# The first two attention tiles on shared weight slots, and the first loads in order

## The reference

```
h   = RMSNorm(x)
one projection of h: q, f, i, g (4 x 512), attention q, k, v (512, 128, 128), two gates (2 x 1024)
A   = HGRN2: S_t = diag(f_t) S_(t-1) + k_t v_t^T, o_t = S_t^T q_t, 4 heads of 128;
      per-head RMS norm, times silu(g)
B   = causal attention over a window of 128, 8 heads of 64 on 2 key heads,
      QK norm, ALiBi, a sink logit in the denominator
x1  = x + (sigmoid(gate_a) * (A @ w_a) + sigmoid(gate_b) * (B @ w_b)) @ w_out
y   = x1 + (gelu(conv3(gate)) * val) @ w_down,   gate, val = RMSNorm(x1) @ w_up  (2 x 2816)
```

## Time and profile before

| | us |
|---|---|
| Runs of the kernel before | 3895.78, 4335.41, 3762.58 (median 3895.78) |
| Profiled execution, time | 3760.1 |
| Its span, slowest of 8 cores | 3758.6 (fastest 3747.6) |
| TensorE busy | 3604.0 (96%) |
| ScalarE, VectorE, POOL busy | 2128.2, 2046.0, 520.6 |
| Moved by DMA | 742.35 MB |

### The profile page before, as it was taken

How to read it: one execution, slowest core, us unless ns; L and a number is a source line. 1 busy time by engine, 2 the same in 40 slices (tenths; PEclk the granted TensorE clock), 3 DMA queues, 4 the chain that set the end, 5 groups by cost and what they waited for, 6 DMA issues and landing times.

```text
span 3758.6 us, 64664 instructions; the slowest of 8 cores (3747.6 to 3758.6 us)
## 1 busy us (share of the span) xinstructions
PE 3604.0 (96%) x21154; PEld 1968.3 (52%) x21516; DVE 2046.0 (54%) x3275; ACT 2128.2 (57%) x3595; POOL 520.6 (14%) x1176
## 2 busy tenths in 40 slices
PE   5779999999999999999999999999999999999999
PEld 2334645546455464654646455464554646456466
DVE  4355455564555646556565555645556465555544
ACT  5567374664746647365483745747375483755722
POOL 1203112010120201102011020201202011020100
PEclk9899999999999999999999999999999999999999
DMA  8879969847465564655646465474655646566464
GB/s 188 180 225 201 258 180 243 257 157 249 143 227 189 181 228 153 222 177 194 225 157 228 161 227 194 159 251 157 205 188 192 230 156 215 178 203 212 136 227 147
DMA packets 205814, 742.35 MB, mean 198 GB/s; under 512 B 22832, under 2 KB 23216, under 8 KB 205488
## 3 DMA queue, kind: packets, MB, share of 16 engines
q1 hardware_dynamic: 191088, 687.95, 54.3%
q0 software_dynamic: 13536, 48.24, 8.2%
q10 hardware_dynamic: 864, 2.00, 0.2%
HBM read 687.76 MB, written 98.57 MB: 209 GB/s over the span
## 4 chain that ended last, share of the span: by engine, by line
PE 86%; ACT 6%; issue 3%; DMA 3%; DVE 1%; POOL 0%; ACTq 0%; another core or an unknown queue 0%; DVEq 0%; SPq 0%; POOLq 0%
PE bank L652 86%; ACT fa L608 2%; DMA wF<-wscr 1%; ACT ef L608 1%; ACT L608 1%; ACT xs L609 1%; DMA wA<-wscr 1%; DMA gB<-c_g 0%; ACT ba L608 0%; DVE fa L630 0%; DMA wF<-wall 0%; DVE ef L625 0%; DMA wA<-wall 0%; PE bank L660 0%; ACT hT L608 0%
## 5 line engine op out<-in xcount | busy, mean ns | idle before, releaser
L652 PE MATMUL bank<-h2T,wF 128*128 128x512 bf16 x5520 | 1282.0, 379 | 40.1 <-ACT ef L608 22.7
L652 PE MATMUL bank<-hT,wA 128*128 128x512 bf16 x4069 | 963.1, 381 | 24.8 <-DMA wA<-wscr 8.4
L652 PEld LDWEIGHTS bank<-h2T,wF 128*128 128x128 bf16 x5632 | 537.0, 98 | 692.4 <-issue 81.3
L625 DVE SCALAR_TENSOR_TENSOR ef<-bank,cft,ef 128x512 f32<-128x512 f32 x704 | 520.7, 747 | 311.8 <-ACT ef L608 265.4
L652 PEld LDWEIGHTS bank<-hT,wA 128*128 128x128 bf16 x4224 | 408.6, 98 | 473.1 <-issue 28.7
L652 PE MATMUL bank<-wF,act 128*128 128x256 bf16 x5632 | 648.9, 273 | 4.2 <-DMA wF<-wscr 4.2
L652 PEld LDWEIGHTS bank<-wF,act 128*128 128x128 bf16 x5632 | 549.1, 98 | 104.0 <-issue 5.5
L608 ACT ACTIVATE ef<-bank,cft 128x512 f32<-128x512 f32 x352 | 273.4, 777 | 327.3 <-PE bank L652 264.4
L630 DVE TENSOR_TENSOR act<-ef,bank 128x512 bf16<-128x512 f32 x352 | 241.5, 686 | 360.4 <-PE bank L652 351.1
L608 ACT ACTIVATE ef<-ef 128x512 f32<-128x512 f32 x352 | 215.4, 627 | 207.4 <-DVE ef L625 205.5
L608 ACT ACT_TABLE_LOAD x235 | 301.5, 1283 | 47.3 <-PE bank L652 31.7
(11 more groups left out here) (87 smaller groups left out, 3358.0 us busy)
## 6 DMA issues: line engine op xcount, KB each, us to landing
wF<-wscr SPq DMA_DIRECT2D x430, 512.0 KB, 4.6
wA<-wscr SPq DMA_DIRECT2D x396, 512.0 KB, 4.9
xt<-x SPq DMA_DIRECT2D x128, 512.0 KB, 7.6
x1scr<-xt SPq DMA_DIRECT2D x64, 512.0 KB, 4.5
xt<-x1scr SPq DMA_DIRECT2D x64, 512.0 KB, 5.8
x<-x1scr SPq DMA_DIRECT2D x64, 512.0 KB, 8.2
y<-x SPq DMA_DIRECT2D x64, 512.0 KB, 6.0
wF<-wall POOLq DMA_DIRECT2D x50, 512.0 KB, 11.8
```

Of the source, the lines that this page charges most:

```text
L625: return P.record("dve", lambda h: h.scalar_tensor_tensor(out=res(out), in0=res(in0), scalar=scalar, in1=res(in1), op0=op0, op1=op1), read ...
L652: inst = h.matmul(res(out), lhsT=res(lhsT), rhs=res(rhs), start=st, stop=sp_)
```

## The change

- Tiles 0 and 1 of stage A use the same weight slots: `load_piece` gives tile 1 the buffer that tile 0 loaded. Tile 1's instructions get priorities from 0.2 on instead of from 1.
- Tile 1's stage A keeps its state in buffers of the MLP (`h2T`, `act`, the x1 pool), as `set1`. `kn` and `vtz` exist twice and alternate. Stage F of tile 0 is recorded after stage A of tile 1, and so on, one behind.
- All pieces of A are copied to `wscr` in tile 0. Of the last four pieces of A three are loaded in tile 0 into the buffers `ef` of the MLP, right after the first gate piece.
- First loads: only cf, cbb and gB0 stay on ScalarE's queue; gB1, mask and dm go to SP's queue, behind certain weight loads. The first two casting loads wait until the first and the second x block have landed.
- Planner: stage A may hold 5 banks instead of 6, `foff` is 0.3 instead of 0.2, priority runs by TensorE cost instead of by count, the small tiles (`sm`) are 6 instead of 5, the score matmuls are costed in full; kt is allocated and recorded ahead of sT.

```diff
-CAPS = dict(pA=6, pF=5)
-TUNE = dict(nxt=4, nxs=4, nwa=5, nwf=5, dA=18, dF=10, dF2=99, rF=1, skew=4, gc=0, foff=0.2, hold=6000.0)
+CAPS = dict(pA=5, pF=5)
+TUNE = dict(xw=1, we=1, le=0, lf=2, nsm=6, rx=0, lj=5, lc=4, a1=0.2, sw=0, gx=0, pm=1.0, dw=1e9, nxt=4, nxs=4, nwa=5, nwf=5, dA=18, dF=10, dF2=99, rF=1, skew=4, gc=0, foff=0.3, hold=6000.0)
...
+            if kind == "A" and ti == 1:
+                base = TUNE["a1"]
+            tot = sum(o.cost for o in ops if o.eng == "pe") or 1.0
+            cum = 0.0
+            m = TUNE["pm"]
             for i, o in enumerate(ops):
-                o.prio = base + i / n
+                o.prio = base + (1.0 - m) * i / n + m * cum / tot
+                if o.eng == "pe":
+                    cum += o.cost
...
-        kn = sb("kn", [128, NB + 1, 128], BF16)
-        vtz = [sb(f"vtz{i}", [128, NB + 1, 128], BF16) for i in range(2)]
+        kn2 = [sb(f"kn{i}", [128, NB + 1, 128], BF16) for i in range(2)]
+        vtz2 = [[sb(f"vtz{i}{j}", [128, NB + 1, 128], BF16) for i in range(2)] for j in range(2)]
...
-        cload("gB1", gB[1][:], c_g[1], 524288)
-        cload("mask", mask_st[:], c_mask, 65536)
-        cload("dm", dm[:], c_dm.rearrange("p a b g t -> p a b (g t)"), 524288)
...
+        set0 = (hT, bhT, qs, bqs, gs, bgs, kd, bkd, vtm, bvtm, qn, bqn, mixT, bmix, gbuf, bgb)
+        set1 = (h2T, bh2T, act[:, 16:20, :], bact[16:20], x1v[0], alias[0], x1v[1], alias[1], x1v[2], alias[2], x1v[3], alias[3],
+                act[:, 0:8, :], bact[0:8], act[:, 8:16, :], bact[8:16])
...
-        keep_at = [(1 if i >= TUNE["dA"] else 0) if p["kind"] == "A" else (2 if i - na >= TUNE["dF2"] else 1 if i - na >= TUNE["dF"] else 0) for i, p in enumerate(pieces)]
+        keep_at = [0 if p["kind"] == "A" else (2 if i - na >= TUNE["dF2"] else 1 if i - na >= TUNE["dF"] else 0) for i, p in enumerate(pieces)]
...
+        def late_const(name):
+            if name == ("q", 0):
+                cload("mask", mask_st[:], c_mask, 65536, eng="sp")
+                P.ops[-1].deps.add(lds[("f", 1)])
+                cload("dm", dm[:], c_dm.rearrange("p a b g t -> p a b (g t)"), 524288, eng="sp")
+            elif name == ("gab", 0):
+                cload("gB1", gB[1][:], c_g[1], 524288, eng="sp")
+                P.ops[-1].deps.add(lds[("g", 1)])
+
         def load_piece(ti, kind, name):
+            if ti == 0:
+                late_const(name)
+            if kind == "A" and ti == 1:
+                return shared[name]
...
+            early = ti == 0 and name in (("wo", 1), ("wo", 2), ("wo", 3)) and TUNE["we"]
+            w = vb(pEF if early else pool, f"w{kind}{ti}_{name}")
...
+            if ti == 0 and name in (("f", 0), ("f", 1)):
+                o_.deps.add(xld[0 if name[1] == 0 else int(TUNE["xw"])])
+            if early:
+                after(o_, lds[("gab", int(TUNE["le"]))])
...
+            hT, bhT, qs, bqs, gs, bgs, kd, bkd, vtm, bvtm, qn, bqn, mixT, bmix, gbuf, bgb = set1 if ti == 1 else set0
+            kn, bkn, vtz, bvtz = kn2[par], bkn2[par], vtz2[par], bvtz2[par]
...
-        for ti in range(ntile):
+        stage_a(0)
+        stage_a(1)
+        stage_f(0)
+        for ti in range(2, ntile):
             stage_a(ti)
-            stage_f(ti)
+            stage_f(ti - 1)
+        stage_f(ntile - 1)
```

More of the change, by code:

```diff
@@ L54 @@
 class VBuf(Buf):
-    __slots__ = ("pool", "slot", "left", "users", "end", "rsv", "cls")
+    __slots__ = ("pool", "slot", "left", "users", "end", "rsv", "cls", "pre")
     def __init__(self, pool, name, rsv=0, cls=""):
@@ L61, in __init__ @@
         self.pool = pool
+        self.pre = ()
         self.slot = None
@@ L68, in __getitem__ @@
     def __getitem__(self, k):
-        return Lz(self, (("g", k),))
+        return Lz(self, self.pre + (("g", k),))
     def lz(self):
@@ L245, in schedule @@
                     st = o.ready
+                    if o.nbytes and dma_free - TUNE["dw"] > st:
+                        st = dma_free - TUNE["dw"]
                     ok = True
@@ L584, in build_program @@
         pBA = mkpool("ba", 6, [T], BF16)
-        pSM = mkpool("sm", 5, [4, 128], BF16)
+        pSM = mkpool("sm", int(TUNE["nsm"]), [4, 128], BF16)
         pEF = mkpool("ef", 3, [2, T + 1], F32)
@@ L720, in build_program @@
         bS32 = mk("S32")
-        bkn = [mk(f"kn{b}") for b in range(NB + 1)]
-        bvtz = [mk(f"vt{b}") for b in range(NB + 1)]
+        bkn2 = [[mk(f"kn{b}") for b in range(NB + 1)] for j in range(2)]
+        bvtz2 = [[mk(f"vt{b}") for b in range(NB + 1)] for j in range(2)]
         bdd = [mk("dd0"), mk("dd1")]
@@ L728, in build_program @@
         for i_ in range(2):
-            P.record("pool", lambda h, i_=i_: h.memset(vtz[i_][:], 1.0), [], bvtz, 700.0)
+            for j_ in range(2):
+                P.record("pool", lambda h, i_=i_, j_=j_: h.memset(vtz2[j_][i_][:], 1.0), [], bvtz2[j_], 700.0)
         for j in range(2):
@@ L745, in build_program @@
         bgd = [mk("gd0"), mk("gd1")]
+        x1v = [a.bitcast(BF16).rearrange("p (a n) -> p a n", a=4) for a in pX1.aps]
+        alias = [[[mk(f"gsx{h}_{b}") for b in range(NB)] for h in range(4)], [mk(f"kdx{h}") for h in range(4)],
+                 [mk(f"vtmx{b}") for b in range(NB)], [[mk(f"qnx{j}_{b}") for b in range(NB)] for j in range(4)]]
+        set0 = (hT, bhT, qs, bqs, gs, bgs, kd, bkd, vtm, bvtm, qn, bqn, mixT, bmix, gbuf, bgb)
+        set1 = (h2T, bh2T, act[:, 16:20, :], bact[16:20], x1v[0], alias[0], x1v[1], alias[1], x1v[2], alias[2], x1v[3], alias[3],
+                act[:, 0:8, :], bact[0:8], act[:, 8:16, :], bact[8:16])
+        x1_users = []
         bgsum = mk("gsum")
@@ L751, in build_program @@
         first_f = {}
+        shared = {}
         na = sum(1 for p in pieces if p["kind"] == "A")
-        keep_at = [(1 if i >= TUNE["dA"] else 0) if p["kind"] == "A" else (2 if i - na >= TUNE["dF2"] else 1 if i - na >= TUNE["dF"] else 0) for i, p in enumerate(pieces)]
-        last_ld = {}
+        keep_at = [0 if p["kind"] == "A" else (2 if i - na >= TUNE["dF2"] else 1 if i - na >= TUNE["dF"] else 0) for i, p in enumerate(pieces)]
+        lds = {}
+        xld = []
         bx1 = {}
@@ L762, in load_piece @@
             pool = pWA if kind == "A" else pWF
-            w = vb(pool, f"w{kind}{ti}_{name}")
+            early = ti == 0 and name in (("wo", 1), ("wo", 2), ("wo", 3)) and TUNE["we"]
+            w = vb(pEF if early else pool, f"w{kind}{ti}_{name}")
+            if early:
+                w.pre = (("r", ("p a n -> p (a n)", {})), ("b", BF16))
             nk = sum(l[3] for l in p["loads"]) if p["loads"][0][3] == 4 and len(p["loads"]) == 2 else p["loads"][0][3]
@@ L766, in load_piece @@
             size = nk * cols
+            if kind == "A" and ti == 0:
+                shared[name] = w
             at = keep_at[i]
@@ L771, in load_piece @@
             o_ = DMA(w[:, 0:size], wall[i, :, 0:size], [], [w], w, size * 512, eng="pool")
-            P.link("al" + kind, o_)
-            last_ld[kind] = o_
+            P.link("alE" if early else "al" + kind, o_)
+            lds[name] = o_
+            if ti == 0 and name in (("f", 0), ("f", 1)):
+                o_.deps.add(xld[0 if name[1] == 0 else int(TUNE["xw"])])
+            if early:
+                after(o_, lds[("gab", int(TUNE["le"]))])
             if kind not in first_f:
@@ L776, in load_piece @@
                 if kind == "F":
-                    after(o_, last_ld["A"])
+                    after(o_, lds[("gab", int(TUNE["lf"]))])
             if ti == at and ntile > at + 1:
@@ L783, in bank, with norm_block @@
             return VBuf(pr[0], "ps", pr[1], pr[2])
-        def norm_block(which, b, xv, hdst, bhdst, pool):
+        def norm_block(ti, which, b, xv, hdst, bhdst, pool):
             st4 = nst[which]
@@ L806, in stage_a @@
             par = ti % 2
+            hT, bhT, qs, bqs, gs, bgs, kd, bkd, vtm, bvtm, qn, bqn, mixT, bmix, gbuf, bgb = set1 if ti == 1 else set0
+            kn, bkn, vtz, bvtz = kn2[par], bkn2[par], vtz2[par], bvtz2[par]
+            kn_o, bkn_o, vtz_o, bvtz_o = kn2[1 - par], bkn2[1 - par], vtz2[1 - par], bvtz2[1 - par]
             for b in range(NB):
@@ L810, in stage_a @@
                 o_ = DMA(xv.lz(), x_d[r0:r0 + 128, :], [], [xv], xv, 524288, chain="xn")
-                after(o_, lead.get(("A", ti - 1)))
+                xld.append(o_)
+                if ti != 1:
+                    after(o_, lead.get(("A", ti - 1)))
                 after(o_, gate.get(ti - int(TUNE["skew"])))
-                norm_block(0, b, xv, hT, bhT, pPA)
+                norm_block(ti, 0, b, xv, hT, bhT, pPA)
             if ti > 0:
-                CP("pool", kn[:, 0, :], kn[:, NB, :], [bkn[NB]], [bkn[0]], n=128)
+                CP("pool", kn[:, 0, :], kn_o[:, NB, :], [bkn_o[NB]], [bkn[0]], n=128)
                 for kv in range(2):
                     vs = slice(kv * 64, (kv + 1) * 64)
```

(29 more changed lines are left out.)

## The result

The changed kernel takes 3788.87 us (median of four runs, 3784.25 to 3793.61). Against the kernel before, each by its comparable runs, the ratio is 1.0075, 95% interval 1.005 to 1.0099: slower, though within 2%. The profiled execution has a span of 3782.7 us, 24 us more than before; I had forecast 3708.

The account below looks back on a forecast made before the run. TensorE bounds the kernel, busy 3604.0 of 3758.6 us. Sixteen steady periods (3629.3 us) plus 19 + 29 + 10 + 10 + 6 + 5 = 79 instead of 129 give span 3708, time 3710 us; range 3675 to 3780.

Parts of the forecast that it names:

- I take 0: Steady periods: the planner's other edits change nothing; ends -1.3 and +5 us a period.
- (d): MLP tiles 0 and 1, 265 to 860 us: idle 10 us above steady instead of 14; ends 5 and 25.
- (a): Start: gB0 at 11 us instead of 18.8, first projection at 23 us instead of 32.98, a gain of 10.
- Rival 2: Steady periods worsen: stage A's bank cap makes TensorE wait in the block part; at 6 us a period 3794; chance 0.1.
- (b): Pair of attention tiles after the first projection: idle 32 us, 29 above steady, against 46; ends 7 and 54.
- My 260 among the signs: Sign for the pair: TensorE busy about 87% from the first projection to 260 us, clock 0.95 or more.
- (c): TensorE's low clock, 28 us before: 10 of the 28 taken for the changed kernel; ends 3 and 25.
- rival 3: Loads hidden anyway: only start and some clock won, MLP tile 0 losing the rest behind casting loads; 3745, chance 0.1.
- (e): The tail, 6 us above steady, to stay; removed transfers stood apart: 9 casting loads and 18 reloads fewer.

Follow-up runs that it names:

- e5: Changed kernel with stage A's bank cap alone put back to 6; ratio to the kernel before 1.0113, lowest run 3807.5 us.
- e13: Changed kernel, same order, each attention block's eight logarithms on 16 of 128 columns, softmax denominators left out; ratio to the kernel before 0.9963, median 3750.95 us.
- e11: Changed kernel with most old planner settings from tile 2 on, and tile 1 loading its own weights; ratio to the kernel before 1.0113, median 3810.38 us.
- e12: Changed kernel with most old planner settings from tile 2 on, and tile 1's norm given priority 0; ratio to the kernel before 1.0008, median 3773.21 us.

## Why the prediction was wrong

**The step that failed is "I take 0" for the planner's other edits**, with the ends -1.3 and +5 a period. It measured +3.4, which is 54 us over 16 periods by my sum, or about 39 over those after 860 us. In that sum the span stands 153 us over sixteen old periods instead of 79: 54 of the 74 us that are missing are this step, some 18 are (d) below, and 4 are (a). I took 0 because idle was already small. But with so little idle an edit had little to win and more to lose, and I had the price of a weak point in reach: 0.36 us for a logarithm in the trace against 0.27 in the code.

**Rival 2 had the sign, the place and nearly the price** (it decides at 3.6 us a period), at a chance of 0.1. Its mechanism was half right. TensorE does wait for banks in the block part, but in e5, with the cap of 6 back, the period stays at 230.8; e13 shows that it hangs on the late logarithms. My own sign for it, a period over 230, came true. It decided earlier than I said, since the start gave less than 50.

(a) Start: gB0 let the first scaling go at 13.51 instead of 18.82, and the first projection began at 26.73; forecast 23, before 32.98. gB0 landed 2.5 us later than I worked out and was still the releaser, after 3.08 us of VectorE's idle; the x blocks came later too. 6 of the 10 us.

(b) Pair: the last output matmuls of attention tile 1 end at 296.8 us. My 260 among the signs did not even follow from my sum, which gives 23 + 216 + 32 + 10 = 281. From the first projection to that end it is 270 us, with TensorE idle for 37, where the sum has 258 and 32. TensorE was busy 84% from 28 to 165 us and 86% in the next 100 us, for my 87%. The size is nearly right, but not the reason. ScalarE is busy there (78 of 100 us), yet the largest gap is at 48 to 62 us:

```profile
48.00:62.00 14.00, 3.37 (x23) 2.37 (x24) 12.66 (x20) 11.74 (x21) 1.09 (x2) 0.57 0.00 0
```

No transfer runs, and TensorE is busy 3.4 of 14 us. All five shared slots hold pieces that tile 0 has used and tile 1 has not, because the last block of tile 1 is not normed: its x block, issued at 24.49 us, had landed by 40, but ScalarE's order squares it only at 52.30. POOL issues the next load only at 68.17 us, when tile 1's first matmuls free a slot. I had counted the transfers that sharing saves and not the slots that it pins. But the pinned slots alone do not explain the gap: in e11, which pins none, the same 14 us have 3.23 busy with a transfer share of 0.77, and TensorE then waits 7.48 us for tile 1's scaling. What both have is the late norm; e12 moved it forward and won 4 of the 14 us.

(c) Clock: 0.95 in both stretches up to 265 us, as I had asked for; the 0.96 from there to 400 us I had not foreseen.

(d) MLP tiles 0 and 1: forecast 4 us better, measured about 14 us worse. This is rival 3's place. The first MLP matmul starts at 329.88 us; it started at 249.42 before. POOL's casting loads, the last at 235.99 us, stop until then:

```profile
321.74 1.40 POOL L640 TENSOR_TENSOR nst<-nst,mhalf 128x1 f32<-128x1 f32 x1 [1.60 <-DVE gsum L640]
...
346.41 0.59 POOL L678 DMA_DIRECT2D wF<-wall  x1 [4.04 <-PE bank L662]
```
```profile
300.00:340.00 40.00, 32.85 (x174) 15.70 (x172) 27.52 (x48) 30.39 (x54) 4.43 (x7) 0.87 0.45 148
320.00:340.00 20.00, 17.54 (x100) 8.87 (x101) 14.95 (x25) 14.73 (x28) 2.10 (x5) 0.75 0.01 2
```

From 320 to 340 us the transfers stand still (share 0.01), and all but five of the MLP's casting loads come after. Yet of TensorE's waits from 265 to 860 us only 3.2 us are for such a load (2.0 before), so it is not, as rival 3 has it, the queue of these loads that costs. Most of the 14 us lie in 300 to 340 us, where the front of attention tile 2 runs almost alone: 7 us of idle, and a clock of 0.87. I had named the lent buffers, which keep MLP tile 0 from filling in there, and priced that at nothing. That they cause the loss is read from the trace; no run took the lent buffers away.

(e) The removed transfers are right: 27 casting loads of A's pieces, 378 reloads, 14 MB less moved. Table loads last 1.28 us here too, with the next activation 1.30 us after (1687.30, 1688.60); no gap stands behind them. The change adds one small tile; my text said two.

## What to carry to other kernels

In a kernel whose order is fixed by a cost model, every edit to its settings is a new order for all tiles; test it apart from the structural change that it comes with, and compare the steady period first. Where the model is wrong about a chain (here eight short activations with a bias from memory, 1.4 us too short), look for orders in which the bottleneck engine waits right behind that chain. When two tiles share a loaded weight, ask when the slower tile lets go of the slot, and what holds that tile up.

## What the runs showed of the hardware

A logarithm of 64 x 128 with a bias lasts 363 ns (changed kernel) and one of 64 x 16 lasts 270 (e13); eight in a row take 3.55 and 2.80 us, so an eighth of the columns saves only a fifth of the time. In the changed kernel the clock of TensorE fell to half after two gaps of 0.46 and 0.99 us within 2 us, in a stretch otherwise nearly fully busy, in six of twelve otherwise equal periods; in e13 the gap of 0.99 us stood alone in eleven of twelve, and the clock never fell there.
